# Head outputs of a two-branch linear-attention layer: frames on the partitions, norms as per-partition sums and scales, tiles transposed back and then gated

## What is computed

```
z = rms_norm(x) @ w_in                    # 10 x 1024 columns: q,k,v,gate of retention; q,f,v,gate of HGRN2; 2 merge gates
o_a = retention(rope(q_a), rope(k_a) / 16, v_a)        # 4 heads, 256 x 256 state
y_a = (silu(g_a) * head_rms(o_a)) @ w_a
o_b = hgrn2(q_b, 1 - f, v_b, log f)                    # 8 heads, 128 x 128 state
y_b = (silu(g_b) * head_rms(o_b)) @ w_b
x   = x + rms_norm((sigmoid(m_a) * y_a + sigmoid(m_b) * y_b) @ w_out)
x   = x + rms_norm(square(relu(rms_norm(x) @ w_up)) @ w_down)
head_rms(o) = o * rsqrt(mean(o * o over the head's width) + 1e-6)
```

## Time and profile before

| | us |
|---|---|
| median of 3 runs | 2622.52 |
| lowest, highest | 2622.17, 2630.27 |
| profiled execution | 2627.63 |
| its span, first to last instruction | 2625.8 |
| TensorE busy | 2549.9 |
| VectorE busy | 1214.7 |
| ScalarE busy | 669.1 |
| GpSimd busy | 446.6 |

### The profile page before, as it was taken

How to read it: one execution, slowest core, us unless ns; L and a number is a source line. 1 busy time by engine, 2 the same in 40 slices (tenths; PEclk the granted TensorE clock), 3 DMA queues, 4 the chain that set the end, 5 groups by cost and what they waited for, 6 DMA issues and landing times.

```text
span 2625.8 us, 38273 instructions
## 1 busy us (share of the span) xinstructions
PE 2549.9 (97%) x14792; PEld 2433.2 (93%) x14792; DVE 1214.7 (46%) x2218; ACT 669.1 (25%) x1257; POOL 446.6 (17%) x656
## 2 busy tenths in 40 slices
PE   7999999999999999999999999999999999999998
PEld 6999999999989989989999999987998998998997
DVE  4043424325366566566576535455333333333335
ACT  5123222322222212212222323233221221221221
POOL 1011102002153353353364200001000000000000
PEclk9999999999999999999999999999999999999999
DMA  4251615234143233223233353322110110110114
GB/s 160 87 180 60 223 61 189 97 105 172 55 155 107 98 92 113 95 89 119 89 98 122 124 186 118 117 91 86 56 57 24 48 56 24 48 56 23 49 40 152
DMA packets 219210, 257.34 MB, mean 98 GB/s; under 512 B 8256, under 2 KB 186816, under 8 KB 218944
## 3 DMA queue, kind: packets, MB, share of 16 engines
q1 hardware_dynamic: 219072, 255.37, 29.5%
HBM read 175.12 MB, written 80.22 MB: 97 GB/s over the span
## 4 chain that ended last, share of the span: by engine, by line
PE 82%; DVE 9%; issue 6%; ACT 1%; DMA 1%; POOL 1%; SPq 0%; DVEq 0%; POOLq 0%; ACTq 0%
PE bank L589 12%; PE bank L591 12%; PE bank L590 12%; PE bank L834 5%; PE bank L836 5%; PE bank L835 5%; PE bank L904 5%; PE bank L905 5%; PE bank L903 5%; DVE PP L1381 2%; PE bank L751 2%; DVE QE L1378 2%; PE bank L862 1%; PE bank L864 1%; PE bank L863 1%
## 5 line engine op out<-in xcount | busy, mean ns | idle before, releaser
L589 PE MATMUL bank<-XH,WHI 128*128 128x384 f32 x2304 | 796.8, 346 | 21.2 <-issue 13.2
L590 PE MATMUL bank<-XL,WHI 128*128 128x384 f32 x2304 | 777.7, 338 | 0.0
L591 PE MATMUL bank<-XH,WLO 128*128 128x384 f32 x2304 | 777.5, 337 | 0.0
L589 PEld LDWEIGHTS bank<-XH,WHI 128*128 128x128 f32 x2304 | 438.9, 190 | 27.9 <-issue 16.5
L590 PEld LDWEIGHTS bank<-XL,WHI 128*128 128x128 f32 x2304 | 439.0, 191 | 1.1
L591 PEld LDWEIGHTS bank<-XH,WLO 128*128 128x128 f32 x2304 | 437.6, 190 | 0.0
L919 ACT ACTIVATE ZST<-bank 128x384 f32<-128x384 f32 x240 | 117.8, 491 | 851.2 <-PE bank L591 850.5
L1213 DVE TENSOR_TENSOR WLO<-WRAW,WHI 128x1024 fp32r<-128x1024 f32 x128 | 171.1, 1336 | 226.2 <-ACT WHI L919 221.0
L834 PE MATMUL bank<-XH,WHI 128*128 128x384 f32 x768 | 257.7, 336 | 3.6 <-ACT XH L919 3.6
L835 PE MATMUL bank<-XL,WHI 128*128 128x384 f32 x768 | 257.5, 335 | 0.0
L836 PE MATMUL bank<-XH,WLO 128*128 128x384 f32 x768 | 257.5, 335 | 0.0
(11 more groups left out here) (184 smaller groups left out, 3342.4 us busy)
## 6 DMA issues: line engine op xcount, KB each, us to landing
scratch_z<-ZST SPq DMA_DIRECT2D x80, 576.0 KB, 2.8
WRAW<-in_w_in SPq DMA_DIRECT2D x80, 512.0 KB, 4.4
HZ<-scratch_z SPq DMA_DIRECT2D x32, 576.0 KB, 4.8
WRAW<-in_w_up SPq DMA_DIRECT2D x32, 512.0 KB, 4.0
WRAW<-in_w_down SPq DMA_DIRECT2D x32, 512.0 KB, 3.4
MG<-scratch_z SPq DMA_DIRECT2D x16, 576.0 KB, 5.8
ZQ<-scratch_z SPq DMA_DIRECT2D x4, 1152.0 KB, 6.3
ZK<-scratch_z SPq DMA_DIRECT2D x4, 1152.0 KB, 8.1
```

The lines of the kernel that those rows point to most:

```text
L589: pe.matmul(psum[c][:, 0:CH], WHI[p][:, k, :], XH[:, k, s], start=(k == 0), stop=False)
L590: pe.matmul(psum[c][:, 0:CH], WHI[p][:, k, :], XL[:, k, s], start=False, stop=False)
L591: last = pe.matmul(psum[c][:, 0:CH], WLO[p][:, k, :], XH[:, k, s], start=False, stop=(k == KT - 1))
```

## The change

The head outputs are made with the frames on the partitions, so that the squares are summed along a partition and the root is one scale per partition.

- `ret_b` and `hg_b` make PO with the scores (128 frames) or the queries stationary and values or state moving: one matmul of 256 columns in place of two of 128 in a retention head, the same number of 128 columns in an HGRN2 head.
- The queries of the sample streams lie in a new buffer QXB, each stream's 16 in a block of 144 columns that are otherwise zero, shifted by 16 frames per stream; a stream's 128 stationary columns hold its queries in its own frames and zeros elsewhere. The matmul then moves its whole state (256 or 128 columns). All of them stand in `ret_b8`, none between the projection's matmuls. GpSimd fills QXB with zeros once.
- Per tile, not per third: ScalarE squares PO with an accumulator output (`head_sq`), VectorE makes the mean (`head_ms`), GpSimd the root (`head_rs`), ScalarE copies PO with the root as scale to OT (`head_scale`, in the next slot, ahead of the slot's eviction), TensorE transposes OT into PRB (`out_t`, a slot after `ret_b` or `hg_b`, between `ret_a` and `ret_b` or `hg_a` and `hg_b` of that slot), VectorE multiplies the transposed tile with the gate into UB (`gated`).
- `head_sum`, `head_spread`, `norm_sum`, the buffers SQ, DG, MS, RST and ones go. SG and UB get a second buffer each; the sigmoids move to slots R_GATE = (8, 9, 14) and H_GATE = (3, 4, 9).
- SyncE's stores of the gated thirds stay where they were and wait for the third's last tile (`um`); GpSimd's order has the roots among the gates and, in an HGRN2 head, inside the key preparation of the last third.
- The program is built with `dynamic_dma_scratch_size=1024`.

```diff
@@ TensorE
-                for e in range(2):
-                    es = slice(e * P, (e + 1) * P)
-                    last = pe.matmul(PO[:, es], kv[:, 0, es], at[:, :], start=(e == 0), stop=(t == 0), skip_group_check=True)
-                    if 0 < t < NT - 1:
-                        for d in range(2):
-                            last = pe.matmul(PO[:, es], SR[:, d, es], QX[:, d, s], start=False, stop=(d == 1), skip_group_check=True)
+                last = pe.matmul(PO[:, 0:RD], at[:, :], kv[:, 0, :], start=True, stop=(t == 0), skip_group_check=True)
+                if t > 0:
+                    for d in range(2):
+                        last = pe.matmul(PO[:, 0:RD], QX[:, d, s], SR[:, d, :], start=False, stop=(d == 1),
+                                         skip_group_check=True)
...
                 for d in range(2):
-                    pe.matmul(PO[:, e * P + b * TS:e * P + (b + 1) * TS], st[:, d, e * P:(e + 1) * P],
-                              QX[:, d, TP + b * TS:TP + (b + 1) * TS], start=(b + d + e == 0), stop=False,
+                    pe.matmul(PO[:, 0:RD], QXB[:, d, b * P:(b + 1) * P], st[:, d, :], start=(b + d == 0), stop=False,
                               skip_group_check=True)
...
+            def out_t(K, h, t, ne):
+
+                pe.wait_ge(K.o_ev, 9 * h + t + 2)
+                pe.wait_ge(K.um, 9 * h + t + 1)
+                if t == NT - 1:
                     pe.wait_ge(K.st_ev, 16 * h + 17)
...
+                for e in range(ne):
+                    last = pe.transpose(PRB[:, e * P:(e + 1) * P], OT[:, e * P:(e + 1) * P], ident[:, :])
+                last.then_inc(K.ot, 1)
...
-                    gemm(8 + 8 * h + j, 4 + 4 * h + j // 2, j % 2, c,
-                         beside=(lambda b: stream_out(h, b, 0)) if s == RA + NT else None)
-                    for i in range(NC):
-                        if s == R_NORM[i]:
-                            head_sum(R, h, i, 2)
-                        if s == R_NORM[i] + 1:
-                            head_spread(R, h, i)
+                    gemm(8 + 8 * h + j, 4 + 4 * h + j // 2, j % 2, c)
+                    if RA <= s < RA + NT:
+                        ret_a(h, s - RA)
+                    if RA + 2 <= s < RA + 2 + NT:
+                        out_t(R, h, s - RA - 2, 2)
@@ ScalarE
+            def head_sq(K, h, t, width):
+
+                act.wait_ge(K.o_full, 9 * h + t + 1)
+                act.activation(OT[:, 0:width], PO[:, 0:width], ACT.Square, accum_out=OSS[:, t:t + 1]).then_inc(K.ss, 1)
+
+            def head_scale(K, h, t, width):
+
+                act.wait_ge(K.rs, 9 * h + t + 1)
+                act.activation(OT[:, 0:width], PO[:, 0:width], ACT.Copy, scale=ORS[:, t:t + 1]).then_inc(K.o_ev, 1)
+
+            def head_gate(K, h, c, ne, gate):
+
+                act.wait_ge(K.um, 9 * h + 1 + (TPC if c == 2 else 0))
+                act.activation(SG[c % 2][:, 0:ne, :], gate, ACT.Sigmoid).then_inc(K.sg, 1)
@@ VectorE
+            def head_ms(K, h, t, width):
+
+                dve.wait_ge(K.ss, 9 * h + t + 1)
+                dve.tensor_scalar(OMS[:, t:t + 1], OSS[:, t:t + 1], 1.0 / width, EPS, ALU.mult, ALU.add).then_inc(K.ms, 1)
+
+            def gated(K, h, t, ne):
+
+                c, r = divmod(t, TPC)
+                rs = slice(r * P, (r + 1) * P)
+                dve.wait_ge(K.ot, 9 * h + t + 1)
...
+                dve.tensor_tensor(UB[c % 2][:, 0:ne, rs], PRB[:, 0:ne * P].rearrange("p (e t) -> p e t", e=ne),
+                                  SG[c % 2][:, 0:ne, rs], ALU.mult).then_inc(K.um, 1)
@@ GpSimd
+            def head_rs(K, h, t):
+
+                pool.wait_ge(K.ms, 9 * h + t + 1)
+                rsqrt(ORS[:, t:t + 1], OMS[:, t:t + 1]).then_inc(K.rs, 1)
...
             def hg_head(h, last):
                 prep_k(h, 1)
+                for c in range(2):
+                    gate(H, h, c, 1, HZ[3][:, c * CH:(c + 1) * CH].unsqueeze(1))
+                head_rs(H, h, 0)
+                head_rs(H, h, 1)
                 pool.wait_ge(H.att, 9 * h + 4)
-                prep_k(h, 2)
-                for c in range(NC):
-                    gate(H, h, c, 1, HZ[3][:, c * CH:(c + 1) * CH].unsqueeze(1))
+                prep_k(h, 2, {1: 2, 4: 3})
+                head_rs(H, h, 4)
+                gate(H, h, 2, 1, HZ[3][:, 2 * CH:].unsqueeze(1))
+                for t in range(5, NT):
+                    head_rs(H, h, t)
```

More of the change, by code:

```diff
@@ L112, in program @@
         ATT = [sb(f"ATT{i}", [P, P], F32, pa) for i in range(2)]
[L113 to L119, removed]
+        SG = [sb(f"SG{i}", [P, 2, CH], F32, pa) for i in range(2)]
+        UB = [sb(f"UB{i}", [P, 2, CH], F32, pa) for i in range(2)]
+        OT = sb("OT", [P, RD], F32, pa)
+        OSS, OMS, ORS = (sb(n, [P, NT], F32, pa) for n in ("OSS", "OMS", "ORS"))
+        QXB = sb("QXB", [P, 2, NS * BW], F32, pa)
         MK = sb("MK", [P, LEV, 64], U32, pa)
@@ L159, in program @@
         SH8 = sb("SH8", [P, NS, HD], F32, ph)
-        KM8 = [(SQ, SG, UB)[b // 3][:, 1, (b % 3) * HD:(b % 3 + 1) * HD] for b in range(NS)]
+        KM8 = [(SG[0], SG[1], UB[0])[b // 3][:, 1, (b % 3) * HD:(b % 3 + 1) * HD] for b in range(NS)]
         URAW = sb("URAW", [P, CH], F32, ph)
@@ L323, in ret_done @@
         def ret_done(e):
-            e.wait_ge(R.u_st, 16 * 3 * RH + 16)
+            for i in range(2):
+                e.wait_ge(R.u_st[i], 16 * (2 - i) * RH + 16)
             e.wait_ge(R.sr_st, 16 * RH + 16)
@@ L330, in hg_done @@
         def hg_done(e):
-            e.wait_ge(H.u_st, 16 * 3 * HH + 16)
+            for i in range(2):
+                e.wait_ge(H.u_st[i], 16 * (2 - i) * HH + 16)
             e.wait_ge(H.sr_st, 16 * HH + 16)
@@ L578, in norm_transpose, with gemm @@
                     last.then_inc(n_tp, 1)
-            def gemm(n, m, p, c, first=False, w=None, part=range(KT), beside=None):
+            def gemm(n, m, p, c, first=False, w=None, part=range(KT)):
                 if c == 0:
@@ L593, in gemm @@
                         last.then_inc(mm, 1)
-                    if beside:
-                        beside(k)
-            for s in (R.rb, H.rb, R.st_full, H.st_full):
+            for s in (R.st_full, H.st_full):
                 pe.sem_inc(s, 1)
@@ L675, in ret_b8 @@
                 pe.wait_ge(R.st_ev, 16 * h + NT)
+                pe.wait_ge(R.o_ev, 9 * h + NT)
+                for i in range(2):
+                    pe.wait_ge(R.s8_in[i], 32 * h + 32)
                 for b in range(NS):
-                    stream_out(h, b, 1)
+                    stream_out(h, b)
                     bank = (PST, PRB)[b % 2]
@@ L977, in block_slot @@
                     whi_block(n + 1, mn, pn)
+                if between:
+                    between()
                 evac(n, m, p, c)
@@ L1023, in _, with between @@
                     j, c = divmod(s, NC)
-                    block_slot(8 + 8 * h + j, 4 + 4 * h + j // 2, j % 2, c)
+                    def between():
+                        if RA + 2 <= s < RA + 2 + NT:
+                            head_scale(R, h, s - RA - 2, RD)
+                        for i in range(NC):
+                            if s == R_GATE[i]:
+                                act.wait_ge(R.g_in[i % 2], 16 * h + 16 if i == 1 else 32 * h + 16 + 8 * i)
+                                head_gate(R, h, i, 2, ZG[i % 2][:, :, :])
+                    block_slot(8 + 8 * h + j, 4 + 4 * h + j // 2, j % 2, c, between)
                     for t in range(NT):
@@ L1345, in _ @@
                             dve.tensor_tensor(ATT[t % 2][:, :], PSC[:, 0:P], DM[:, t // NTP, :], ALU.mult).then_inc(R.att, 1)
+                    if RA + 2 <= s < RA + 2 + NT:
+                        gated(R, h, s - RA - 2, 2)
+                    for t in range(NT):
                         if s == RA + 1 + t and t < NT - 1:
@@ L1634, in _ @@
                 last.then_inc(R.k_ok, 1)
-                for c in range(NC):
-                    gate(R, h, c, 2, ZG[c % 2][:, :, :])
+                for c in range(2):
+                    gate(R, h, c, 2, ZG[c][:, :, :])
+                for t in range(NT):
+                    head_rs(R, h, t)
+                    if t == 4:
+                        gate(R, h, 2, 2, ZG[0][:, :, :])
                 ch.reset()
@@ L1643, in _, with prep_k @@
             ch.reset()
-            def prep_k(h, c):
+            def prep_k(h, c, after={}):
                 s = slice(c * CH, (c + 1) * CH)
```

173 lines of the change are left out of this document (64 added, 109 removed).

## The result

The changed kernel takes 2554.8 us (median of four runs, 2553.6 to 2556.5) beside 2623.7 for the kernel before (2622.2 to 2630.3): a ratio of 0.9743, 95% interval 0.9730 to 0.9756. It is 69 us faster. The profiled executions are 71.1 us apart (2627.6 and 2556.5).

A forecast was written before the change was run, and what follows sets the result against it. TensorE, busy 97% and 82% of the chain, was taken as the bound, with VectorE setting one HGRN2 stretch. 18 + 12.6 + 9.6 = 40 us off the 2622.5 median gave 2583 us; eight in ten between 2566 and 2604.

The forecast's parts named there:

- Passes in the retention heads: TensorE, four retention heads: sums and spreads go, transposes come, outputs and streams get cheaper; 4.5 us per head, 18 us.
- (d): TensorE: a pass costs by the columns it moves, narrow ones nearly free; slower, 2641 us; chance 0.02.
- Passes in slots 6 to 12 of HGRN2: TensorE, slot 4 to slot 13's projection: two sums and two spreads go, eight transposes come; 12.6 us over eight heads.
- VectorE's stretch from slot 13 to slot 4: HGRN2, slot 13 to the next head's slot 4, set by VectorE's queue: 1.3 us for seven heads, 9.6 with the end.
- term of contention: HGRN2, before tile 0: GpSimd's two gate multiplies run beside VectorE's weight split and slow it; 0.4 us lost a head.
- the clock at 0: TensorE's half-clock stretches after slot-4 waits: waits stay as long, so no gain from the clock, bound +-5 us.
- (b): HGRN2 slot 4: the waits shrink, and with them the stretches at 1.2 GHz, 11 + 8 us; 2563 us; chance 0.08.
- (a): HGRN2 slots 6 to 9: the new chain is late, or contention takes back the second stretch; 2600 us; chance 0.12.
- (c): All slots: transposes wait for square, mean, root and copy across four engines; 1 us per tile gives 2690 us; chance 0.06.
- The margin: Time to spare before TensorE's transpose needs the scaled tile: about 2 us, least in HGRN2 slots 7 and 8, about 1.

The follow-up runs named there:

- written-out pair: Both kernels with TensorE's loops over retention heads and HGRN2 pairs and VectorE's over pairs written out: 2599.7 us (kernel before), 2539.5 us (changed kernel).
- split first: Changed kernel with the second query rotation of a retention head moved from slot 1 to slot 3 on VectorE, behind the weight split: 2549.9 us, 0.9713.
- three roots: Changed kernel with each head root on GpSimd done three times in a row: ratio 0.9746.
- both paddings: Changed kernel with 192 or 96 semaphore increments that nobody waits for in TensorE's retention loop: 2568.9 us (192), 2563.8 us (96).

## Why the prediction was wrong

**Passes in the retention heads: right.** 18.6 us for 18; padded queries cost what narrow ones did, and passes of one column were worth as much as those of 128, so (d) is out. **Passes in slots 6 to 12 of HGRN2: somewhat low.** 17.1 for 13.5, or for 12.6 with the eighth transpose. A slot that loses a sum or a spread and gets a transpose fell by 0.55 to 0.61 us, where 0.48 and 0.53 were forecast, and a slot with only the new transpose grew by 0.04 to 0.07 us, not 0.11.

**The step that failed first: no term for the loop's turn.** The prediction said that TensorE's queue waits once in each HGRN2 head and took the one row of its waits that fits. The row "L589 <- issue: 13.2, 6, 3.6" stood in the same list and got no term. Three stops of 3.6 us and the half clock behind them were 17.3 us; the edit shortens the body, and they went. 6.6 came back as late splits of slot 6, which the stop had covered: the question "what is late next" was asked of the new waits only, not of these stops. Net 10.7.

**The second: VectorE's stretch from slot 13 to slot 4, 1.3 us a head.** In the written-out pair TensorE gets to the transposes of slot 4 2.6 us earlier (34.25 and 31.65 us after the start of slot 13, mean of seven heads): 0.55 at the forget step (0.5 said), 1.23 for the multiplies (1.2 said), and 0.81 won in the other instructions where I had 0.4 lost. So it was the term of contention that had the wrong sign. Its reason was wrong too: GpSimd's early gates come behind the split, not beside it (at 917.6 us in the head whose split ends at 914.6). That split took 1.30 to 1.39 us in the changed kernel, and 1.23 to 1.49 before, not 1.63. Over the heads, with the end of the last one and the clock, 20.3 us for 9.6 in the pair.

**The third: the clock at 0.** I let the waits stay as they are the earlier trace rows. They fell to 13.7, since VectorE's side won more than TensorE's 1.2 a head, and through the shorter stop at VectorE's turn. The stretches at half clock in the HGRN2 heads went from 34 to 17 us in sum, which gives back 8.5 in this pair of executions; the longest is now this (length, busy us of the engines, granted clock):

```profile
1100.60:1107.30 6.70, 6.70 (x28) 6.70 (x29) 2.05 (x9) 1.10 (x4) 2.10 (x3) 0.50 0.16 49
```

The 17 us are not a steady figure: versions of the changed kernel with the same 13.6 to 13.9 us of waits show 20, 27, 31 and 31 (split first, three roots, both paddings). The form of the kernel with its loops adds 3.9 to the pair's 20.3, which makes the 24.2 of the table.

The sum, a bookkeeping of these traces: 40.2 forecast, 0.6 and 4.5 for passes, 10.7 for the pair's stretch, 3.9 for turns and clock in HGRN2, 10.7 for the turns in retention: 70.6 of 71.1.

**The rivals.** (b), with 0.08, named the place, nearly its size and nearly the time (2563): the waits at slot 4 fell by 8.8 us where it had 11, and the half clock gave back 8.5 where it had 8. Its cause, VectorE's times beside GpSimd, is the 0.8 us a head above; the stops at VectorE's turn, shorter by 2.6 us in sum, it didn't name, and the 10.7 in retention are outside it; its time is 8 us too long. (a) and (c) are out: the chain of square, mean, root and copy is nowhere late, and contention took nothing back. The margin was given as 1 us in slots 7 and 8; it is 1.6 or more, and as small in slots 12 and 13. In slot 12 ScalarE makes eight masked key copies ahead of the square, and TensorE has no next tile's first half to do.

## What to carry to other kernels

A row "issue" among the waits of the engine that sets the time is a place to look, not a remainder: find the stops, and if they stand at a loop's turn, count the engine's instructions in the body. The chain's share of that name was no guide here; it didn't follow the stops. An edit that takes instructions out can then pay twice, and the same stop written out of the program pays by itself. Where two engines share a stretch that sets the time, the durations of one trace don't simply add: a row of 27 us moved by 0.8 to 1.1 us (mean of seven heads) beyond the instructions taken out or put in. Give such a term bounds on both sides, and add the half clock that follows each wait.

## What the runs showed of the hardware

- A loop body of 1706 recorded instructions on TensorE turned without a stop or a fetched packet; one of 1802 stopped at one turn of three (5.3 us); 1898 and 1905 at each (3.5 to 3.6 us, up to 6.8 us at half clock behind). The kernel before with that loop as straight code fetched 97 packets for 102 and had no stop in these heads.
- VectorE's stop at its own turn was 1.8 to 2.0 us in the changed kernel, 3.0 to 3.3 in the kernel before, 3.1 to 3.4 with SP's store held back, and 2.0 to 2.4 in two runs on the kernel before whose store of z landed sooner after the stop began.
- A semaphore increment between two projection matmuls cost TensorE nothing measurable: slots of 4.16 us with and without eight of them.
- A multiply of 128x192 on VectorE took 0.36 to 1.05 us in the same place of the program, by what GpSimd ran beside it.
